# Attention scores of two heads in the two row halves of TensorE, with the small jobs of the auxiliary bank moved inside the projection units

## The reference, cut to what matters

```python
# A: sliding window (128), 8 query heads on 2 key heads, head width 64, a learned sink per head
s = jnp.einsum('bnqkgd,bnskd->bnkgqs', qb, kb).astype(jnp.float32) * (hd ** -0.5)
m = jnp.maximum(jnp.max(s, axis=-1, keepdims=True), sink)
p = jnp.exp(s - m)
denom = jnp.sum(p, axis=-1, keepdims=True) + jnp.exp(sink - m)
# B: MoBA, 8 heads of width 64; with 256 tokens and blocks of 256 it is plain causal attention
s_own = jnp.einsum('bhqd,bhsd->bhqs', qs, k_own).astype(jnp.float32) * scale
p = jax.nn.softmax(jnp.concatenate([s_sel, s_own], axis=-1), axis=-1)
# C: Mamba-2 SSD: conv, dt, sums of dt*a, C.B products, states, gated group norm
```

## Time and profile before

| | before |
|---|---|
| median of 3 runs | 1229.36 us (1227.92 to 1229.87) |
| the profiled execution's own time | 1228.32 us |
| its span in the trace | 1226.6 us |
| TensorE busy | 1182.6 us, 96% |
| VectorE busy | 761.9 us, 62% |
| ScalarE busy | 587.8 us, 48% |
| GpSimd busy | 86.4 us, 7% |
| transfers, mean busy share of 16 engines | about 51% |

### The profile page before, as it was taken

The page is one execution under the profiler, slowest core; times in us unless marked ns, Lnnn a source line. Parts: engine busy times, 40 slices in busy tenths (PEclk is TensorE's granted clock), DMA queues, the critical chain, the costliest instruction groups (busy, mean ns, idle before and its releaser), DMA issues.

```text
span 1226.6 us, 18296 instructions
## 1 busy us (share of the span) xinstructions
PE 1182.6 (96%) x7502; PEld 1059.5 (86%) x7502; DVE 761.9 (62%) x1144; ACT 587.8 (48%) x832; POOL 86.4 (7%) x119
## 2 busy tenths in 40 slices
PE   2999999999999999999989999999999999999997
PEld 1998899999898888888879888999999987888886
DVE  3776766685745456555568667567675544666554
ACT  4544544545454354444445554545554544544442
POOL 4000001420000000000020000023100000000000
PEclk9999999999999999999999999999999999999999
DMA  6652534547554445565636444266556453565561
GB/s 154 203 167 74 181 124 139 172 147 261 188 168 134 143 162 180 192 210 172 204 93 221 138 139 137 78 182 203 185 174 210 138 169 107 172 211 172 192 227 41
DMA packets 155419, 201.31 MB, mean 164 GB/s; under 512 B 6096, under 2 KB 110920, under 8 KB 155336
## 3 DMA queue, kind: packets, MB, share of 16 engines
q1 hardware_dynamic: 155208, 200.08, 50.4%
q0 software_dynamic: 128, 0.06, 0.3%
HBM read 199.04 MB, written 1.08 MB: 163 GB/s over the span
## 4 chain that ended last, share of the span: by engine, by line
PE 87%; DVE 4%; ACT 3%; issue 2%; DMA 2%; POOL 2%; SPq 0%; DVEq 0%; POOLq 0%; ACTq 0%
PE psum L1059 10%; PE psum L1060 10%; PE psum L1061 10%; PE psum L1068 10%; PE psum L1070 10%; PE psum L1069 10%; PE psum L1049 10%; PE psum L1050 5%; PE psum L1132 2%; PE psum L1173 2%; PE psum L1145 1%; PE psum L1218 1%; DMA raw<-in_w_br_moba_dram 1%; PE psum L1195 1%; DVE w_lo L1362 1%
## 5 line engine op out<-in xcount | busy, mean ns | idle before, releaser
L1362 DVE TENSOR_TENSOR w_lo<-raw,w_hi 128x2048 fp32r<-128x2048 f32 (+1 forms) x184 | 418.4, 2277 | 253.5 <-ACT w_hi L725 253.5
L725 ACT ACTIVATE w_hi<-raw 128x2048 fp32r<-128x2048 f32 (+2 forms) x188 | 347.8, 1858 | 110.1 <-PE psum L1070 86.9
L1059 PE MATMUL psum<-act_both,w_hi 128*128 128x256 f32 x832 | 240.7, 289 | 0.0
L1060 PE MATMUL psum<-act_both,w_hi 128*128 128x256 f32 x832 | 235.9, 283 | 0.0
L1061 PE MATMUL psum<-act_both,w_lo 128*128 128x256 f32 x832 | 235.8, 283 | 0.0
L1049 PE MATMUL psum<-act_both,w_hi 128*128 128x512 f32 x512 | 181.8, 399 | 0.3 <-DVE w_lo L1362 0.2
L1059 PEld LDWEIGHTS psum<-act_both,w_hi 128*128 128x128 f32 x832 | 160.1, 192 | 1.1 <-issue 0.5
L1060 PEld LDWEIGHTS psum<-act_both,w_hi 128*128 128x128 f32 x832 | 160.2, 193 | 0.6 <-issue 0.5
L1061 PEld LDWEIGHTS psum<-act_both,w_lo 128*128 128x128 f32 x832 | 159.9, 192 | 0.0
L1050 PE MATMUL psum<-act_both,w_lo 128*128 128x256 f32 x512 | 143.5, 280 | 0.0
L1049 PEld LDWEIGHTS psum<-act_both,w_hi 128*128 128x128 f32 x512 | 96.2, 188 | 25.2 <-DVE w_lo L1362 1.0
(11 more groups left out here) (250 smaller groups left out, 1995.0 us busy)
## 6 DMA issues: line engine op xcount, KB each, us to landing
raw<-in_w_in_dram SPq DMA_DIRECT2D x36, 1024.0 KB, 5.3
raw<-in_w_up_dram SPq DMA_DIRECT2D x32, 1024.0 KB, 5.4
raw<-in_w_down_dram SPq DMA_DIRECT2D x32, 1024.0 KB, 5.0
raw<-in_w_gate_dram SPq DMA_DIRECT2D x24, 1024.0 KB, 7.1
raw<-in_w_ckv_dram SPq DMA_DIRECT2D x16, 1024.0 KB, 5.3
raw<-in_w_br_ssd_dram SPq DMA_DIRECT2D x8, 1024.0 KB, 9.8
raw<-in_w_mix_out_dram SPq DMA_DIRECT2D x8, 1024.0 KB, 5.0
raw<-in_w_cq_dram SPq DMA_DIRECT2D x8, 1024.0 KB, 5.3
```

What stands on the lines that cost most here:

```text
L725: ins = act.activation(w_hi[:, slot, cut], raw[:, slot, cut], ACT.Copy)
L1059: pe.matmul(dst, m_hi[:, k, cs], a_hi[:, k, :], start=k == 0, stop=False)
L1060: pe.matmul(dst, m_hi[:, k, cs], a_lo[:, k, :], start=False, stop=False)
L1362: dve.tensor_tensor(w_lo[:, slot, 0:n], raw[:, slot, 0:n], w_hi[:, slot, 0:n].bitcast(F32), ALU.subtract).then_inc(lo_ready.sem, 1)
```

## The change

Two edits that belong together. First, a job takes two neighbouring heads (2j and 2j + 1): they lie in the same tile, one in rows 0 to 63, one in rows 64 to 127, and each writes its scores to a bank of its own, 4 and 5. Second, the turned probabilities, which had bank 5, go to the auxiliary bank 7. The other users of bank 7 up to slot 24 leave the end of slot u and go into the middle of unit u + 1 (`inner`, called between m = 0 and m = 1, or between t = 0 and t = 1); on VectorE and ScalarE their readers stand ahead of the job's work in iteration u + 1.

```diff
-ACS_SLOT, BTOK_SLOT, CB_SLOT, STATES_SLOT = U_XBC[3], U_XBC[4] + 2, U_XBC[5] + 3, U_XBC[5] + 6
-XS_SLOTS = (U_Z[0] + 1, U_XBC[5] + 2)
+ACS_SLOT, BTOK_SLOT, CB_SLOT, STATES_SLOT = U_XBC[3] + 1, U_XBC[4] + 3, U_XBC[5] + 4, U_XBC[5] + 6
+XS_SLOTS = (U_Z[0] + 2, U_XBC[5] + 3)
...
-    return 4 * (j // 2) + j % 2 + 2 * i
+    return 2 * j + i
...
+TURN_SLOT = [s + (2 if i < 3 else 1) for i, s in enumerate(CLOSE_SLOT)]
...
     if 0 <= job_at(s) < SSD_JOB0:
-        out.append((SB_, ("score", job_at(s))))
+        out += [(SB_, ("score", job_at(s), 0)), (TB_, ("score", job_at(s), 1))]
     if 0 <= job_at(s - 1) < SSD_JOB0:
-        out.append((TB_, ("probsT", job_at(s - 1))))
+        out.append((YB_, ("probsT", job_at(s - 1))))
...
                     for m in range(n // P):
+                        if m == 1:
+                            inner(l, u)
...
                     for t in tiles:
+                        if t == 1:
+                            inner(l, u)
...
+            def inner(l, u):
+                if u == ACS_SLOT:
...
+                if u == CB_SLOT:
...
+                if u == BTOK_SLOT:
...
+                if u in XS_SLOTS:
+                    g = XS_SLOTS.index(u)
+                    pe.wait_ge(*xbc_ready.at(l, 4))
+                    for t in range(TT):
+                        key = ("xs", g, t)
+                        pe.wait_ge(*is_free(l, key))
+                        for k in range(4):
+                            ins = pe.transpose(bank(key)[:, k * P:(k + 1) * P],
+                                               xbcT[:, 4 * g + k, t * P:(t + 1) * P], ident[:])
+                        ins.then_inc(full(key), 1)
+                for i in range(3):
+                    if u == TURN_SLOT[i]:
+                        close_turn(l, i)
...
                 for i in range(2):
-                    q_tile = head_of(j, i) // 2
-                    k_tile = 4 + (j // 2 if branch == 0 else q_tile)
-                    ins = pe.matmul(bank(key)[:, i * 2 * P:i * 2 * P + (t + 1) * P],
-                                    qk[half_p, q_tile, t * P:(t + 1) * P], qk[half_p, k_tile, 0:(t + 1) * P],
-                                    start=True, stop=True)
-                ins.then_inc(full(key), 1)
+                    key = ("score", n, i)
+                    half_p = slice(i * HD, (i + 1) * HD)
+                    pe.matmul(bank(key)[:, 0:(t + 1) * P], qk[half_p, j, t * P:(t + 1) * P],
+                              qk[half_p, k_tile, 0:(t + 1) * P], start=True, stop=True).then_inc(full(key), 1)
```

More of the change, by code:

```diff
@@ L193 @@
 CLOSE_SLOT = [job_slot(c[0]) + 2 for c in CLOSINGS]
+TURN_SLOT = [s + (2 if i < 3 else 1) for i, s in enumerate(CLOSE_SLOT)]
+INNER_SLOTS = (ACS_SLOT, BTOK_SLOT, CB_SLOT) + XS_SLOTS + tuple(TURN_SLOT[:3])
+assert len(set(INNER_SLOTS)) == len(INNER_SLOTS)
 SB_, TB_, OB_, YB_ = 4, 5, 6, 7
@@ L228, in slot_banks @@
         out += [(YB_, ("xs", XS_SLOTS.index(s), 0)), (SB_, ("xs", XS_SLOTS.index(s), 1))]
+    for i in range(3):
+        if s == TURN_SLOT[i]:
+            out.append((YB_, ("closeT", i)))
+    if s == SWA_T_SLOT:
+        out += [(b, ("qkT", i)) for i, b in enumerate((SB_, TB_, OB_))]
+    if 0 <= job_at(s) < SSD_JOB0:
+        out += [(SB_, ("score", job_at(s), 0)), (TB_, ("score", job_at(s), 1))]
+    if 0 <= job_at(s - 1) < SSD_JOB0:
+        out.append((YB_, ("probsT", job_at(s - 1))))
+    if job_at(s - 2) in [0, 4, 8, 12, 16, 18, 20, 22]:
+        out.append((OB_, ("values", job_at(s - 2))))
     if s == STATES_SLOT:
@@ L233, in slot_banks @@
             out.append((YB_, ("yoff", group)))
-    for i in range(8):
-        if s == CLOSE_SLOT[i] + 1:
+    for i in range(3, 8):
+        if s == TURN_SLOT[i]:
             out.append((YB_, ("closeT", i)))
@@ L939, in _ @@
                         out_of_bank(l, ("btok",), b_tok[:].rearrange("p k n -> p (k n)"), bank(("btok",))[:, 0:SEQ])
+                    for i in range(3):
+                        if u == TURN_SLOT[i]:
+                            close_hi_part(l, i)
+                    if u == ACS_SLOT:
+                        act.wait_ge(*decay_arg.at(l, 1))
+                        act.activation(decay[:], decay[:], ACT.Exp).then_inc(decay_exp.sem, 1)
+                    turned_probs(l, job_at(u - 1))
                     if u == STATES_SLOT:
@@ L943, in _ @@
                             out_of_bank(l, ("states", g), states[:, g, :])
-                    for i in range(8):
-                        if u == CLOSE_SLOT[i] + 1:
+                    for i in range(3, 8):
+                        if u == TURN_SLOT[i]:
                             close_hi_part(l, i)
@@ L1120, in job_scores @@
                 branch, t, j = job_of(n)
-                key = ("score", n)
                 if n == 0:
@@ L1254, in _ @@
                         job_values(l, job_at(u - 2))
[L1255 to L1291, removed]
@@ L1582, in job_mask @@
                 branch, t, j = job_of(n)
-                key = ("score", n)
                 if n < SSD_JOB0:
-                    dve.wait_ge(*is_full(l, key))
+                    for i in range(2):
+                        dve.wait_ge(*is_full(l, ("score", n, i)))
                 else:
@@ L1606, in job_mask @@
                 for i in range(2):
[L1607 to L1614, removed]
+                    c, key = i * 2 * P, ("score", n, i)
+                    dve.tensor_tensor_reduce(s_sb[:, n % 2, c:c + keys], bank(key)[:, 0:keys], mask, 1.0,
+                                             -3.0e38, ALU.add, ALU.max, row_max[:, i:i + 1]).then_inc(free(key), 1)
+                for i in range(2):
+                    dve.wait_ge(*is_read(l, ("score", n, i)))
                 if branch == 0:
                     c = PC_SINK + head_of(j, 0)
-                    steps.link(dve.tensor_tensor(row_max[:], row_max[:], par[:, c:c + 3:2], ALU.max))
+                    steps.link(dve.tensor_tensor(row_max[:], row_max[:], par[:, c:c + 2], ALU.max))
                 h = HEADS * t + head_of(j, 0)
-                dve.tensor_scalar(neg_max[:, branch, h:h + 3:2], row_max[:], -ATT_SCALE, None, ALU.mult)\
+                dve.tensor_scalar(neg_max[:, branch, h:h + 2], row_max[:], -ATT_SCALE, None, ALU.mult)\
                    .then_inc(masked.sem, 1)
@@ L1712, in _ @@
                     h = u - CROSS_SLOT0
+                    if u == ACS_SLOT:
+                        sums_of_adt(l)
+                    if u in XS_SLOTS:
+                        xs_tokens(l, XS_SLOTS.index(u))
+                    for i in range(3):
+                        if u == TURN_SLOT[i]:
+                            close_lo_part(l, i)
                     if 0 <= job_at(u):
                         job_mask(l, job_at(u))
-                    if u == ACS_SLOT:
-                        sums_of_adt(l)
                     if u == DT_SLOT:
                         softplus_dt(l)
[L1719 to L1722, removed]
+                    for i in range(3, 8):
+                        if u == TURN_SLOT[i]:
                             close_lo_part(l, i)
```

42 lines of the change are left out of this document (30 added, 12 removed).

## The result

The changed kernel takes 1221.97 us (median of 6 runs, 1220.31 to 1223.55) against 1229.28 for the kernel before on the same chip (6 runs); the ratio of the runs is 0.9948, with a 95% interval of 0.9935 to 0.9962 (the two medians by themselves give 0.9941, inside it). On a second chip it took 1221.49 against 1228.06, ratio 0.9948 (0.9933 to 0.9964).

The account below looks back on a forecast made before the run. TensorE, almost never idle in the attention slots, was taken to bound the kernel. 3.4 us saved on bursts less 1.8 of waits gave -1.6 us, a median of 1227.8 us against 1229.36; 8-in-10 range 1224.3 to 1231.6.

Parts of the forecast that it names:

- The burst of scores: A job's score products on TensorE: one of four passes saved, 0.21 us with 256 keys, nothing with 128; 3.4 us.
- the sum: Waits of TensorE from the moves at slots 17, 18 and 15: 0.9 us per layer, 1.8 in all.
- The fixed 0.22 us of a burst: Part of each burst of scores on TensorE that does not depend on the number of keys: 0.22 us.
- Slot 17: Scores of job 10 wait for bank 4 until VectorE's `xs` operations, now behind a `w_lo`, are done: 0.6 us.
- Slot 18: Turn of job 10 waits for bank 7 until VectorE's `ya_lo`, now behind the convolution, is done: 0.27 us extra.
- the old wait: Slot 18 before the change: the turn waited for the exponentials; forecast to go, with a longer wait in its place.
- Slot 15: Turn of job 7 needs bank 7 about when VectorE has read the sums, now behind the convolution: 0.05 us.
- The other 0.3 us: Moves outside slots 15, 17 and 18: forecast to find cover, and moved transposes and sums to cost TensorE the same time.
- Rival 2: Score bursts: no overlap of the two heads' passes, only the waits stay; +1.8, 1231.2 us; chance 13%.
- Rival 3: VectorE gets to `xs` and `ya_lo` in time, so no waits; -3.4 to -5.1, 1226.0 to 1224.3 us; chance 12%.
- Rival 1: 128-key bursts gain too, as loads of two halves overlap; 1.3 more, -2.9, 1226.5 us; chance 28%.
- Rival 4: Switching row halves drains the array, each of 32 bursts grows by 0.1 us; +5.0, 1234.4 us; chance 9%.

Follow-up runs that it names:

- a, a, b, b: Changed kernel with each score product issued twice, both of head a's before both of head b's; 1232.90 us, one run.
- same_half: Changed kernel with a job's two heads put back into the same row half, all moves kept; 1230.37 us, 1.0024 of the kernel before.
- mended_exps: Changed kernel with three VectorE readers put earlier (sums, `xs` of group 0, `ya_lo`) and ScalarE's exponentials ahead of the tanh in xbc units; 1216.07 us, ratio 0.9904.
- doubled couples: Changed kernel with every score product issued twice, in order a, b, a, b (1234.46 us) or a, a, b, b (1232.90 us), one run each.
- mended_xs: Changed kernel with only the `xs` operations of group 0 put ahead of the `w_lo` of unit 19 on VectorE; 1225.42 us, one run.
- apart: Changed kernel with the second head's score product put behind the turn of the job before, so 128-row transposes stand between; 1247.77 us, one run.

## Why the prediction was wrong

**What bounds the kernel.** Right. TensorE set the time in the attention slots before and after, and the length of the slots shows every wait there, and every shorter burst that no wait ate.

**The burst of scores: the step that failed.** The prediction said: "If matmuls start in order, only pass 2 of a can lie beside pass 1 of b: one of four passes is saved." The runs show no such order between the halves: with a, a, b, b the eight passes took the time of four. The next sentence failed too: "With 128 keys I take nothing, since the loading of weights seems to bind there". Loads may well set the pace within one half; but two halves load at once. So the term that was put at 3.4 us is 16 x 0.22 + 16 x 0.43 = 10.4 us. It was given 5.1 as its upper bound, and the true size lay beyond it, because the bound rested on the same assumption as the value. None of the rivals had it; the last sentence of the prediction only named it as a way to be wrong ("if a burst shrinks by more than one pass"). Against the 10.4 us the waits and the longer units took 4.2, where the sum had 1.8, so the slots shrank by 6.2 us in all instead of 1.6. The fixed 0.22 us of a burst stayed fixed. The rule that matmuls keep program order was read in the Trainium skill, page "TensorE: Matmul & The Clock Gate", Part 3; within one half nothing here speaks against it, between two halves the trace doesn't bear it out. Its other part, that matmuls of different row groups run side by side, the trace confirms: a couple takes 0.63 us, and so does one head alone.

**The moves: mechanism right, size too small.** The waits came at the three slots named, ended by the operations named. Without the overlap (same_half) they are 1.51 us per layer, where the sum had 0.92. Slot 17: 0.6 forecast, 0.5 measured. In the changed kernel it reads just as worked out, the `xs` operations directly behind the `w_lo`:

```profile
134.80 2.29 DVE L1380 TENSOR_TENSOR w_lo<-raw,w_hi 128x2048 fp32r<-128x2048 f32 x1
137.01 0.68 DVE L1711 TENSOR_TENSOR xdt<-psum,dt_sb 128x512 f32<-128x512 f32 x1
...
138.81 0.68 DVE L1713 TENSOR_TENSOR xd_sb<-psum,par 128x512 f32<-128x512 f32 x1
```

TensorE's scores start as soon as the last of them is over:

```profile
139.54 0.49 PE L1189 MATMUL psum<-qkT_b 64*128 64x128 f32 x4 [0.46 <-DVE xd_sb L1713]
```

Slot 18: 0.27 more than the old wait forecast, 1.52 - 1.06 = 0.46 in same_half. Slot 15: 0.05 forecast, 0.85 - 0.64 = 0.2 there. The other 0.3 us were forecast as nothing. The small operations themselves take no longer inside a unit (the eight `xs` transposes 0.79 us, before 0.80), but the unit that they split does: that of `closeT` 0 takes 2.96 + 3.05 = 6.01 us in same_half and 5.92 in the kernel before.

**The waits grow with the gain.** In the changed kernel's timeline the bursts of slots 15 and 18, each up to the turn behind it, read:

```profile
122.88 0.49 PE L1189 MATMUL psum<-qkT_b 64*128 64x128 f32 x4
123.77 0.63 PE L1200 MATMUL psum<-ident,s_sb 128*128 128x128 f32 x4 [0.40 <-DVE decay L1697]
...
146.76 0.49 PE L1189 MATMUL psum<-qkT_b 64*128 64x128 f32 x4
148.32 0.41 PE L1200 MATMUL psum<-ident,s_sb 128*128 128x128 f32 x2 [1.07 <-DVE ya_lo L1681]
```

That is 0.89 and 1.56 us where 0.42 is the rule: waits of 0.47 and 1.14. Where VectorE sets the turn, a shorter burst only lengthens the wait: it is 0.2 us in slot 15 of same_half and 0.47 here. Per layer the bursts give 8 x 0.22 + 8 x 0.43 = 5.2 us; of these 0.47 (slot 15), 0.5 (slot 17), 1.14 - 0.42 = 0.72 (slot 18, less its old wait), 0.11 (slot 21, a burst of 0.74) and the 0.3 of split units go back. This leaves 3.1, and 3.12 were measured.

**The rivals.** Rival 2 (no overlap, only the waits, +1.8) is what same_half shows, at +3.0 in the slots. Rival 3 (no waits) did not come by itself; mended_exps, with another order on VectorE and ScalarE, has no waits, and is 10.7 us shorter in the slots than the kernel before. Rival 1's reason, loads in two halves at once, was right. Rival 4's, a drain between the halves, was wrong: the passes of the halves come in pairs, 6 ns apart.

## What to carry to other kernels

Put two products that contract over 64 rows into different row halves, directly behind one another: here, in f32, with 128 or 256 columns and a bank for each, the second was free, doubled couples took the same in either order, and the transposes over 128 rows between them cost all of it and 0.2 us per couple more. When small readers are moved to another place, look at what long operation now stands before them on their engine; here three readers on VectorE that stood behind a `w_lo` or a convolution cost 1.8 us per layer, which another order got back, and the exponentials behind the tanh on ScalarE, for which TensorE waited before the change too, another 0.43. When a bound is worked out from an assumption, take a bound that survives the assumption: here half of a burst's passes.

## What was not expected of the hardware

- Two 64-row products in different halves, weight loads included, run at once: a couple takes 0.63 us with 256 columns and 0.42 with 128, as one head's product alone does, and doubled couples take 1.07 and 0.64 to 0.66 in either order.
- In mended_xs a wait of 2.36 us, in both layers, was followed by about 3 us at half of the clock (0.50), which cost 1.5 us, more than the 1.29 us by which the wait was longer than the changed kernel's 1.07; behind that one the clock stayed at 1.00.
- The length of one wait does not settle it: in the first layer of apart waits of 0.76 us (slot 15) and 1.24 us (slot 18) were each followed by a clock of 0.50, and in its second layer waits of 0.76 and 1.21 us in the same slots were not. What does settle it stays open.
